# The last gate of a decoder layer: six prompt tiles multiplied in pairs by seven half-size products each

## The reference

```
x = x + (silu(h @ w_gate) * (h @ w_up)) @ w_down            # feed-forward, width 2816
x = x + sigmoid(rms_norm(x, norm_ple) @ w_ple_gate) * (pe @ w_ple_proj)
```

## Time and profile before

| | us |
|---|---|
| median of 3 runs | 1666.63 (1666.49 to 1666.73) |
| the profiled execution | 1666.75 |
| its span on the core | 1664.6 |
| PE busy in the span | 1637.4 (98%) |
| DVE, ACT, POOL busy | 1233.1, 672.4, 526.4 |

### The profile page before, as it was taken

How to read it: one execution, slowest core, us unless ns; L and a number is a source line. 1 busy time by engine, 2 the same in 40 slices (tenths; PEclk the granted TensorE clock), 3 DMA queues, 4 the chain that set the end, 5 groups by cost and what they waited for, 6 DMA issues and landing times.

```text
span 1664.6 us, 28928 instructions
## 1 busy us (share of the span) xinstructions
PE 1637.4 (98%) x10629; PEld 1475.0 (89%) x10629; DVE 1233.1 (74%) x1875; ACT 672.4 (40%) x1270; POOL 526.4 (32%) x345
## 2 busy tenths in 40 slices
PE   9999999999999999999989999999999999999998
PEld 8999887777999999878889999999999888888886
DVE  6387876777999999876897777777776676954544
ACT  6303366765544444643462233333222335442111
POOL 2304695421656656621233222222221000700000
PEclk9999999999999999999999999999999999999999
DMA  6401000001432222230215444444444877662101
GB/s 197 139 1 50 15 1 0 1 26 36 132 91 59 63 67 71 65 108 1 77 32 174 146 146 146 146 146 146 146 146 154 287 267 242 194 225 68 46 33 48
DMA packets 155919, 172.37 MB, mean 104 GB/s; under 512 B 35156, under 2 KB 107377, under 8 KB 155679
## 3 DMA queue, kind: packets, MB, share of 16 engines
q1 hardware_dynamic: 153955, 170.52, 31.6%
q10 hardware_dynamic: 1860, 0.51, 0.1%
HBM read 130.54 MB, written 40.80 MB: 103 GB/s over the span
## 4 chain that ended last, share of the span: by engine, by line
PE 83%; DVE 11%; issue 2%; POOL 1%; ACT 1%; SPq 1%; DMA 0%; ACTq 0%; DVEq 0%; POOLq 0%
PE ps L2717 22%; PE ps L2719 22%; PE ps L2718 22%; DVE arena L2282 2%; DVE arena L1856 2%; PE ps L3185 1%; PE ps L3007 1%; PE ps L2980 1%; PE ps L2723 1%; PE ps L2724 1%; PE ps L637 1%; PE ps L2960 1%; POOL stats L1001 1%; PE ps L2966 1%; DVE pT_lo L2173 1%
## 5 line engine op out<-in xcount | busy, mean ns | idle before, releaser
L1159 POOL TENSOR_TENSOR arena<-arena,mhalf 128x32 f32<-128x32 f32 (+1 forms) x40 | 180.6, 4522 | 114.1 <-DVE arena L2287 114.1
L2717 PE MATMUL ps<-cw_hi,pT_hi 128*128 128x288 f32 x512 | 164.0, 320 | 1.3 <-DVE pT_lo L2173 0.8
L1856 DVE SCALAR_TENSOR_TENSOR arena<-arena,tapw 128x1024 f32<-128x1024 f32 x120 | 159.6, 1330 | 1.8
L2491 DVE TENSOR_TENSOR dn_lo<-dn_raw,dn_hi 128x1024 fp32r<-128x1024 f32 x83 | 116.9, 1420 | 58.2 <-ACT dn_hi L1759 57.4
L2717 PE MATMUL ps<-T_hi,S_hi 128*128 128x272 f32 x528 | 152.3, 288 | 3.0 <-issue 1.3
L2719 PE MATMUL ps<-T_hi,S_lo 128*128 128x272 f32 x528 | 151.9, 288 | 0.0
L2718 PE MATMUL ps<-F_B_r,S_hi 128*128 128x272 f32 x528 | 151.8, 287 | 0.0
L2718 PE MATMUL ps<-cw_lo,pT_hi 128*128 128x288 f32 x512 | 150.8, 294 | 0.0
L2719 PE MATMUL ps<-cw_hi,pT_lo 128*128 128x288 f32 x512 | 150.7, 294 | 0.0
L1759 ACT ACTIVATE dn_hi<-dn_raw 128x1024 fp32r<-128x1024 f32 x83 | 87.6, 1060 | 131.8 <-DMA dn_raw<-in_w_down 62.3
L2717 PE MATMUL ps<-dn_hi 128*128 128x512 f32 x308 | 120.0, 390 | 0.2 <-DVE U L2410 0.2
(11 more groups left out here) (438 smaller groups left out, 4808.9 us busy)
## 6 DMA issues: line engine op xcount, KB each, us to landing
dn_raw<-act_mid SPq DMA_DIRECT2D x77, 256.0 KB, 2.8
arena<-in_cache_ckv SPq DMA_DIRECT2D x128, 128.0 KB, 2.0
dn_raw<-in_w_down SPq DMA_DIRECT2D x45, 256.0 KB, 3.5
w_raw<-in_w_gate SPq DMA_DIRECT2D x22, 512.0 KB, 3.8
w_raw<-in_w_up SPq DMA_DIRECT2D x22, 512.0 KB, 4.8
arena<-in_w_down SPq DMA_DIRECT2D x22, 512.0 KB, 6.5
act_mid<-arena SPq DMA_DIRECT2D x11, 1024.0 KB, 8.2
wt_mid<-arena SPq DMA_DIRECT2D x11, 1024.0 KB, 4.2
```

Of the source, the lines that this page charges most:

```text
L1159: nc.gpsimd.tensor_tensor(rstd_k[:, g0:g1, :], ms_k[:, g0:g1, :], mhalf[:, 0:(g1 - g0) * NH].rearrange("p (g h) -> p g h", h=NH), ALU.pow) ...
L1856: ins = nc.vector.scalar_tensor_tensor(y_of(c), glu[:, c, k:k + SEQ], tapw[:, c, k:k + 1], y_of(c), ALU.mult, ALU.add)
L2491: nc.vector.tensor_tensor(dn_lo_r[s], dn_raw[s], dn_hi[s][0], ALU.subtract).then_inc(s_("a_split"), 1)
L2717: mm(out, left[0], right[0], start=start, stop=False)
```

## The change

The sample tile comes second (PLE_TILES = 2, sample, 3, 4, 5, 0, 1, 6, 7). The first three tiles (`PLAIN = 3`) are computed as before; the other six go in three pairs, (4, 5), (0, 1), (6, 7). With A the normalised rows of a pair (each of its tiles a half-row of blocks, split in the middle of the contraction) and B the gate weights in four blocks of 512 x 512, a pair takes seven products, each 4 contraction steps x 3 matmuls over 512 columns:

```diff
+PLAIN = 3
+TWINS = [(PLAIN + 2 * q, PLAIN + 2 * q + 1) for q in range((NT - PLAIN) // 2)]
+G_PRODUCTS = ["P1", "P6", "P2", "P5", "P7", "P3", "P4"]
+G_LEFT = {"P1": "A11", "P6": "S2", "P2": "A12", "P5": "S1", "P7": "S3", "P3": "S4", "P4": "A22"}
+G_RIGHT = {"P1": "B11", "P6": "T2", "P2": "B21", "P5": "T1", "P7": "T3", "P3": "B22", "P4": "T4"}
+            def gate_product(q, name):
+                left, right = G_LEFT[name], G_RIGHT[name]
+                pe.wait_ge(s_("h4_split"), G_LOWS(q, left))
...
+                for k in range(KH):
+                    last = split_mm(ps[:, G_BANK[name], :], (a[0][:, k, :], a[1][:, k, :]), (G_B[right][0][:, k, :], G_B[right][1][:, k, :]),
+                                    start=k == 0, stop=k == KH - 1)
```

The weight sums T1 to T4 are made once, by POOL, a quarter of the contraction (k) at a time, during the ring; SP stores each quarter (1 MB) to DRAM in the ring's steps 46, 52, 58 and 65 and loads T2, T1, T3 (1 MB each) when the ring's last slots come free and T4 when the third gate product is done. POOL's low halves of the gate weights, which overwrite the operands of the sums, now follow the last store:

```diff
+            for k in range(KC // 2):
+                if k >= 1:
+                    pool.wait_ge(s_("mid_stored"), T_STORED(k - 1))
+                t_sum(k, "T1", w_pg[0][:, k, HALF:DM], w_pg[0][:, k, 0:HALF])
+                pool.wait_ge(s_("sum_ready"), T_SUMMED(k, "T1"))
+                t_sum(k, "T2", w_pg[1][:, k, HALF:DM], t_sums[:, 0, :])
+                t_sum(k, "T3", w_pg[1][:, k, HALF:DM], w_pg[0][:, k, HALF:DM])
+                pool.wait_ge(s_("sum_ready"), T_SUMMED(k, "T2"))
+                t_sum(k, "T4", w_pg[1][:, k, 0:HALF], t_sums[:, 1, :])
+            pool.wait_ge(s_("mid_stored"), T_STORED(KC // 2 - 1))
             pool.wait_ge(s_("w_high"), len(W_ORDER) + 3)
             for k in range(KC // 2):
                 low_pg(0, k)
...
+                for k in range(KC // 2):
+                    if i == dn_first("P4") + (2, 8, 14, 21)[k]:
+                        sp.wait_ge(s_("sum_ready"), T_SUMMED(k, "T4"))
+                        sp.dma_start(t_mid[k].rearrange("b p n -> p b n"), t_sums).then_inc(s_("mid_stored"), 16)
```

PE's order in a pair, and where it waits:

```diff
+            for q, (u, v) in enumerate(TWINS):
...
+                gate_product(q, "P2")
+                gate_product(q, "P5")
+                if more:
+                    pe.wait_ge(s_("c_hT"), G_GAINED(v))
+                    nt_pe(pe, "c", NT + u + 3, P, xn4, 0)
+                pe.wait_ge(s_("c_done"), G_MADE(q, "U2"))
+                gate_product(q, "P7")
+                if more:
+                    pe.wait_ge(s_("c_hT"), G_GAINED(u + 2))
+                    nt_pe(pe, "c", NT + v + 3, P, xn4, 0)
+                proj_tile(u)
+                pe.wait_ge(s_("c_done"), G_MADE(q, "V5"))
+                gate_product(q, "P3")
+                pe.wait_ge(s_("c_done"), G_MADE(q, "U3"))
+                gate_product(q, "P4")
+                proj_tile(v)
```

ACT's gain of a pair's first tile, its rounding of T4 ahead of it, and DVE's low halves of the weight sums:

```diff
+                    for k in range(KH):
+                        g = COLS["norm_ple"][0] + KH * b + k
+                        last = nc.scalar.activation(G_full[0][("A11", "A12")[b]][0][:, k, :], ps[:, b, k * P:(k + 1) * P], ACT.Copy, scale=gcol[:, g:g + 1])
...
+                gate_of(q, "C11")
+                if q == 0:
+                    high_t("T4")
+                if more:
+                    gain_u(q + 1)
...
+            def low_t(name):
+                dve.wait_ge(s_("w_high"), T_HIGH(name))
+                nc.vector.tensor_tensor(T_full[name][1], T_full[name][0], T_hi[name][0], ALU.subtract).then_inc(s_("b_dve"), 1)
```

More of the change, by code:

```diff
@@ new lines, in x_scale, with gain_v @@
+            def x_scale(j):
+                m = rows_of(PLE_TILES[j])
+                nt_dve_scale(dve, "c", NT + j + 1, x2[0:m, PLE_TILES[j], :], m, G_COL(j), xn4)
+            def gain_v(q):
+                j = TWINS[q][1]
+                dve.wait_ge(s_("c_xT"), NT + j + 1)
+                for b in range(2):
+                    g0 = COLS["norm_ple"][0] + KH * b
+                    last = nc.vector.tensor_tensor(G_full[q % 2][("A21", "A22")[b]][0], ps[:, b, :].rearrange("p (k c) -> p k c", c=P),
+                                                   gcol[:, g0:g0 + KH].unsqueeze(2).to_broadcast([P, KH, P]), ALU.mult)
+                last.then_inc(s_("c_hT"), 1)
+                dve.wait_ge(s_("c_hT"), G_GAINED(j))
@@ new lines, in sum_a4 @@
+            def sum_a4(q, name):
+                a, b, op = {"S1": ("A21", "A22", ALU.add), "S2": ("S1", "A11", ALU.subtract), "S3": ("A11", "A21", ALU.subtract),
+                            "S4": ("A12", "S2", ALU.subtract)}[name]
+                f = G_full[q % 2]
+                if name in ("S2", "S4"):
+                    dve.wait_ge(s_("s_sums"), G_SUMMED(q, b if name == "S4" else a))
+                if name == "S4" and q >= 1:
+                    dve.wait_ge(s_("prod_done"), G_DONE(q - 1, "P3"))
+                nc.vector.tensor_tensor(f[name][0], f[a][0], f[b][0], op).then_inc(s_("s_sums"), 1)
@@ new lines, in low_a4, with result_4 @@
+            def low_a4(q, name):
+                dve.wait_ge(s_("b_high"), G_HIGHS(q, name))
+                full = G_full[q % 2][name]
+                nc.vector.tensor_tensor(g_lo_a11 if name == "A11" else full[1], full[0], G_hi[name][0], ALU.subtract).then_inc(s_("h4_split"), 1)
+            def result_4(q, name):
+                p, base, out = {"U2": ("P6", sg[:, 0:HALF], g_u2), "C11": ("P2", sg[:, 0:HALF], sg[:, 0:HALF]), "V5": ("P5", g_u2, g_v5),
+                                "C22": ("P7", g_v5, sg_v[:, HALF:DM]), "U3": ("P7", g_u2, g_u2), "C12": ("P3", g_v5, sg[:, HALF:DM]),
+                                "C21": ("P4", g_u2, sg_v[:, 0:HALF])}[name]
+                if name == "U2":
+                    dve.wait_ge(s_("p1_copied"), PAIRS + q + 1)
+                elif name in ("V5", "C22", "C21"):
+                    dve.wait_ge(s_("c_done"), G_MADE(q, {"V5": "U2", "C22": "V5", "C21": "U3"}[name]))
+                dve.wait_ge(s_("prod_done"), G_DONE(q, p))
+                nc.vector.tensor_tensor(out, base, ps[:, G_BANK[p], :], ALU.add).then_inc(s_("c_done"), 1)
@@ new lines, in end_4 @@
+            def end_4(q, name):
+                i, h = "uv".index(name[0]), int(name[1])
+                j, w = TWINS[q][i], slice(h * HALF, (h + 1) * HALF)
+                g = (sg, sg_v)[i]
+                if name in (G_ENDS[q][0], G_ENDS[q][2]):
+                    dve.wait_ge(s_(f"y_stored{j % 2}"), 16 * (j // 2))
+                dve.wait_ge(s_("sg_ready"), G_GATED(q, {"u0": "C11", "u1": "C12", "v0": "C21", "v1": "C22"}[name]))
+                dve.wait_ge(s_("pp_done"), PLAIN + 2 * (j - PLAIN) + h + 1)
+                ch.link(nc.vector.tensor_tensor(g[:, w], g[:, w], ps[:, 5 + h, :], ALU.mult))
+                nc.vector.tensor_tensor(y_out[j % 2][:, w], g[:, w], x2[:, PLE_TILES[j], w], ALU.add).then_inc(s_("y_ready"), 1)
@@ L2689, in _ @@
+            for j, t in enumerate(PLE_TILES[0:PLAIN]):
+                nt_dve_mean(dve, "c", NT + j + 2, rows_of(PLE_TILES[j + 1]), 0)
+                x_scale(j + 1)
+                if j == 1:
+                    low_t("T2")
                 if t == TILES:
@@ L2700, in _ @@
                     dve.wait_ge(s_(f"y_stored{j % 2}"), 16 * (j // 2))
[L2701 to L2706, removed]
+                gated(j, (0, 1), j + 1)
+                low_p(j + 1)
+            for name in G_LOW[2:]:
+                low_a4(0, name)
+            for q, (u, v) in enumerate(TWINS):
+                more = q + 1 < len(TWINS)
+                result_4(q, "U2")
+                if more:
+                    nt_dve_mean(dve, "c", NT + u + 3, P, G_COL(u))
+                    x_scale(u + 2)
+                    nt_dve_mean(dve, "c", NT + v + 3, P, G_COL(v))
+                result_4(q, "C11")
+                result_4(q, "V5")
+                if more:
+                    dve.wait_ge(s_("c_xT"), NT + u + 3)
+                    x_scale(v + 2)
+                if q == 0:
+                    low_t("T4")
+                result_4(q, "C22")
+                result_4(q, "U3")
+                if more:
+                    gain_v(q + 1)
+                    for name in ("S1", "S2", "S3"):
+                        sum_a4(q + 1, name)
+                    low_a4(q + 1, "A11")
+                end_4(q, "u0")
+                low_p(v)
+                result_4(q, "C12")
+                if more:
+                    sum_a4(q + 1, "S4")
+                end_4(q, "u1")
+                if more:
+                    low_a4(q + 1, "S2")
+                    low_a4(q + 1, "A12")
+                result_4(q, "C21")
+                if more:
+                    for name in ("S1", "S3", "S4"):
+                        low_a4(q + 1, name)
+                for name in G_ENDS[q][2:]:
+                    end_4(q, name)
+                if more:
+                    low_p(u + 2)
+                    low_a4(q + 1, "A22")
         @block.tensor
@@ L3366, in _, with gate_tile @@
                     p_T(0)
-            for j, t in enumerate(PLE_TILES):
+            def gate_tile(j):
+                t = PLE_TILES[j]
                 r = rows_of(t)
@@ new lines, in _ @@
+            for j in range(PLAIN):
+                gate_tile(j)
+                if j + 1 < PLAIN:
```

(26 more changed lines are left out.)

198 lines of the change are left out of this document (171 added, 27 removed).

## The result

| kernel | median us | against the runs of before beside it |
|---|---|---|
| before | 1666.66 (1666.31 to 1668.00, 7 runs) | |
| changed | 1672.03 (1667.74 to 1672.46, 7 runs) | 1.0027 [1.0017, 1.0037] |

The change makes the kernel slower by 5.4 us, where 4.25 us less was forecast, in a range from 1659.2 to 1665.9. The profiled execution took 1672.03, span 1670.2.

The account below looks back on a forecast made before the run. PE, busy 98% of the span, was taken to bound the kernel with its matmuls. Saved matmuls -8.15, tile order 0, PE waits on DVE +1.2, ring +2.7 gave -4.25 us: 1662.4 us for the median, range 1659.2 to 1665.9.

Parts of the forecast that it names:

- The weight sums in the ring: Ring, P3's end and P2's start: late POOL low halves take turns with DVE subtractions; PE loses 2.7 us (0.7 to 4.1).
- Step 71's subtraction: Ring, P3's end: five turns after step 66's subtraction, this one ends 0 to 3.4 us late for PE.
- the store also holds up the loads of steps 66 and 67: Ring: the fourth store of sums delays these two loads; reason given for taking 2.7 us, above the middle.
- In P2's first four steps ... another 0.2 each, 0.7: Ring, P2's start: a turn of 3.35 us against 14 matmuls, 3.17, costs 0.2 us per step, 0.7 in all.
- in that stretch it made 11 ... and PE didn't wait: P4's stretch before the change: DVE made 11 subtractions where PE used 12 steps; the ring's lead covered it.
- The matmuls and the pairs: Last stage: three pairs save 36 matmuls, -8.15 us; PE waits on DVE cost 1.2 us (0.5 to 3.5).
- tile 3's middle transposes: Tile 3's gate product: transposes of the first pair's first tile need its scaled rows from DVE; PE waits 0.5 us.
- the 0.7 before the first pair's second transposes: First pair: DVE needs 7.1 us until these may overwrite the banks, PE has 6.4 us of work; PE waits 0.7.
- Tile order, transfers, end: Sample tile's new place, T loads and the last half's multiply, add and store: each costs 0.
- VectorE becomes the bound of the pairs: Rival, chance 0.07: DVE operations in the pairs run longer and PE waits; 20% longer adds 8.3 us, 1670.7.
- The ring costs more than the sums suggest: Rival, chance 0.20: turns of 3.64 us or a store of 9 us or longer; 5 to 6 us in the ring, 1665.3.
- No stall in the ring: Rival, chance 0.17: the ring's leads cover the turns, as they did at 1412; 1659.7 us.

Follow-up runs that it names:

- experiment 2: Kernel before with one wait added: POOL starts its ten low halves when ring step 62 is done, no weight sums or stores; 1677.49 us.
- experiment 1: Changed kernel with POOL's ten low halves spread between its groups of weight sums instead of behind the last store; 1660.49 us.
- experiment 3: Changed kernel with P3's sample additions moved ahead of the subtraction for step 74 in DVE's queue, low halves still late; 1670.24 us.
- experiment 4: Changed kernel with six low halves between the weight sums and the four of the gate's second half behind the last store; 1660.63 us.
- experiment 5: Changed kernel with low halves spread between the weight sums, but low_pg(1, 1) and low_pg(1, 2) behind the fourth group, not the third; 1659.55 us.
- experiment 6: Changed kernel with low halves still late, each made by two POOL instructions of 512 columns instead of one of 1024; 1660.34 us.

## Why the prediction was wrong

**The step that failed is "The weight sums in the ring".** Its term was 2.7 us (0.7 to 4.1); the ring lost 12.4. Point by point:
- Where POOL's low halves land was forecast right (from 1472 to 1477 until 1506 to 1510; measured 1475.4 to 1507.8), and the turn (3.35 forecast, 3.25 measured).
- Step 71's subtraction, "0 to 3.4 us late", was right: PE waited 2.6 us for it. The remark that "the store also holds up the loads of steps 66 and 67" was right too: the five turns began behind a subtraction for step 66 that came 3.2 us later than before. In experiment 2, without the store, that subtraction came at 1475.46 and six turns made PE wait 2.1 us; in experiment 1, with the same store but low halves that end at 1473.7, PE did not wait at step 71 at all.
- "In P2's first four steps ... another 0.2 each, 0.7" was wrong. It counted subtractions against matmuls and forgot that DVE's queue holds P3's additions as well, behind three subtractions, and that PE's P2 needs these additions ten matmuls into its first step. Three turns of 3.25 from 1495.7 put them at 1505.5, five us after P3's end. The trace of before would have shown that these additions had 0.2 to 0.3 us to spare. Experiment 2 shows this wait without the sums (5.6 us), experiment 3 shows it move with the place in the queue.
- The reasoning "in that stretch it made 11 ... and PE didn't wait" carried the absence of waits in P4's middle over to a stretch with a change of product. Experiment 1 met the same thing at the change from P4 to P3.
- The clock was no term at all. I took the earlier trace rows's 0.2264 for every matmul; 17 ran at 0.43 behind the waits, 3.4 us.

**The matmuls and the pairs:** -8.15 + 1.2 = -6.95 was forecast, -6.86 measured (-6.85 to -6.90 in experiments 1, 4, 5, 6). The sum held, its parts less so: of the waits of 1.2 only 0.2 to 0.3 is at tile 3's middle transposes (0.5 forecast), and the 0.7 before the first pair's second transposes is not among the waits: there PE started 0.37 instead of 0.23 after the matmul ahead. In its place each pair takes a little longer than counted. PE's first matmul behind the same transposes in two successive pairs:

```profile
1598.57 0.48 PE L2999 MATMUL ps<-t_hi_T,g_hi_S 128*128 128x512 f32 x1
...
1625.79 0.48 PE L2999 MATMUL ps<-t_hi_T,g_hi_S 128*128 128x512 f32 x1
```

27.2 us for a pair where 26.7 was counted; the starts are 0.24 to 0.32 us apart at the first matmuls of products and in some steps, without a wait that the trace names. That the sum came so close is luck in part: a wait that did not come was made up by slower starts that nobody had counted.

**Tile order, transfers, end:** 0, as forecast; the 0.6 us behind the sample tile is there in both.

**The rivals:** "VectorE becomes the bound of the pairs" is refuted, since no wait in a pair is over 0.3 us. "The ring costs more than the sums suggest" had the right place, but with 5 to 6 us and with another cause: its longer turn or later store, where the turn was 3.25 us and the store landed as forecast. "No stall in the ring" gave 1659.7, and that is where the kernel stands once its low halves are elsewhere (1659.55).

**Open:** what decides whether the granted clock falls. It fell behind waits of 4.3 and 5.6 us and behind 1.85 that followed 2.31; behind 2.58 it fell in the changed kernel, behind 2.59 in experiment 3 it did not, nor behind 2.07 in experiment 2.

## What to carry to other kernels

A wait that a slower engine causes is found by walking that engine's whole queue, not only the kind of instruction that is slowed: look where another engine needs what is queued behind, above all where the work changes from one product to the next, and read how much room it had there before. When work is moved to wait for a transfer, ask what it will run beside at its new time; small pieces between the waits, or shorter instructions, cost little or nothing here where one late block cost 12 us. Behind stalls of 2 to 6 us count on a possible stretch of TensorE work at half speed too, which here cost up to half as much again as the stalls.

## What the runs showed of the hardware

- POOL and DVE subtractions, both with two SBUF operands, take turns of 3.25 us with 1024 columns each and 2.0 us with 512 on POOL; both are shorter than the two alone one after the other (3.64 and 2.52).
- DVE additions with one operand in PSUM kept their 0.67 to 0.69 us beside POOL's subtractions, as in the earlier trace rows.
- The granted clock fell to its lower level behind PE's waits of 2.58, 4.30 and 5.63 us and behind one of 1.85 that followed one of 2.31, for 3.2 to 5.5 us of work; behind waits of 2.07 and 2.59 us, and of 0.4 and 0.8, it stayed at 1.00.
